# A triangular solution in other temporaries, with the log-decay chain amid its steps, and value, key and gate tiles in another order

## What is computed

```python
proj = h @ w_in
gq, gk, gv, g_low, rw, gate = jnp.split(proj, SPLIT0, axis=-1)
log_decay = jax.nn.log_sigmoid((g_low @ gk_up + gk_bias)) / 16.0
b = jnp.cumsum(g in chunks of 64)                  # GLA decay
q * jnp.exp(b - ref), k * jnp.exp(ref - b)         # ref: middle of the chunk
...
S = S * w_t + sa * b_t + v_t * k_t                 # RWKV-7, token by token
...
o = jnp.concatenate([o_a, o_b]) * jax.nn.silu(gate)
return o @ w_out
```

## Time and profile before

| | us |
|---|---|
| median of three executions | 1244.69 |
| lowest, highest | 1243.75, 1245.27 |
| the profiled execution, its own time | 1252.05 |
| its span, first to last instruction | 1249.8 |
| busy: PE, DVE, ACT, POOL | 1124.4, 662.6, 332.7, 294.0 |
| mean granted TensorE clock | 0.95 of full |

### The profile page before, as it was taken

How to read it: one execution, slowest core, us unless ns; L and a number is a source line. 1 busy time by engine, 2 the same in 40 slices (tenths; PEclk the granted TensorE clock), 3 DMA queues, 4 the chain that set the end, 5 groups by cost and what they waited for, 6 DMA issues and landing times. The chain is left out here.

```text
span 1249.8 us, 20321 instructions
## 1 busy us (share of the span) xinstructions
PE 1124.4 (90%) x8408; PEld 899.1 (72%) x8408; DVE 662.6 (53%) x1031; ACT 332.7 (27%) x749; POOL 294.0 (24%) x190
## 2 busy tenths in 40 slices
PE   3999999999964578898889997999999899998997
PEld 3777777888753468787734446888888788887886
DVE  5288898499995315344434115255510258987233
ACT  6333423101103314233241003011110224554121
POOL 2222322334331011010000004133322534440500
PEclk9999999999987799999989998999999959999999
DMA  5211211632111060200204201111111010131011
GB/s 193 68 51 35 53 49 41 214 101 84 34 51 67 18 186 3 70 3 3 70 1 184 102 34 63 51 42 42 50 50 34 35 51 18 35 133 34 17 51 68
DMA packets 37577, 77.77 MB, mean 62 GB/s; under 512 B 19184, under 2 KB 19712, under 8 KB 37120
## 3 DMA queue, kind: packets, MB, share of 16 engines
q1 hardware_dynamic: 27616, 66.23, 15.9%
q10 hardware_dynamic: 9888, 10.49, 2.6%
HBM read 59.93 MB, written 16.78 MB: 61 GB/s over the span
## 5 line engine op out<-in xcount | busy, mean ns | idle before, releaser
L1383 PE MATMUL ps<-HNH,WH 128*128 128x512 f32 x896 | 356.2, 398 | 51.1 <-ACT GV L508 25.8
L1383 PE MATMUL ps<-HNH,WL 128*128 128x512 f32 x896 | 352.4, 393 | 0.0
L1383 PE MATMUL ps<-HNL,WH 128*128 128x512 f32 x896 | 352.0, 393 | 0.0
L1383 PEld LDWEIGHTS ps<-HNH,WH 128*128 128x128 f32 x896 | 170.4, 190 | 89.9 <-issue 54.4
L1383 PEld LDWEIGHTS ps<-HNH,WL 128*128 128x128 f32 x896 | 170.8, 191 | 36.3 <-issue 1.2
L1383 PEld LDWEIGHTS ps<-HNL,WH 128*128 128x128 f32 x896 | 170.6, 190 | 36.4
L1282 PE MATMUL ps<-BK,SG 128*128 128x512 f32 x256 | 112.8, 601 | 1.4 <-PEq L787 1.4
L1282 PEld LDWEIGHTS ps<-BK,SG 128*128 128x128 f32 x256 | 49.3, 193 | 63.7 <-issue 63.7
L1744 ACT ACTIVATE GV<-GV,nm 128x256 f32<-128x256 f32 x128 | 64.3, 504 | 78.6 <-DVE nm L1765 78.3
L666 DVE TENSOR_TENSOR VQ<-GV 128x62 f32<-128x62 f32 (+30 forms) x62 | 71.4, 1152 | 20.2 <-DMA GV<-bonds_dram 18.1
L1704 PE MATMUL ps<-V,GV 128*128 (+1 forms) x512 | 73.2, 292 | 0.8 <-DVE GV L1778 0.7
(11 more groups left out here) (246 smaller groups left out, 1728.9 us busy)
## 6 DMA issues: line engine op xcount, KB each, us to landing
GV<-in_w1t SPq DMA_DIRECT2D x18, 512.0 KB, 3.6
AR<-in_x SPq DMA_DIRECT2D x16, 512.0 KB, 7.1
WA<-in_w0t SPq DMA_DIRECT2D x16, 512.0 KB, 3.6
RAW<-in_w0t SPq DMA_DIRECT2D x8, 512.0 KB, 3.7
gate_dram<-RAW ACTq DMA_DIRECT2D x8, 512.0 KB, 2.6
SG<-gate_dram SPq DMA_DIRECT2D x1, 4096.0 KB, 15.4
BK<-in_wout SPq DMA_DIRECT2D x4, 1024.0 KB, 6.8
h_dram<-H SPq DMA_DIRECT2D x8, 512.0 KB, 2.6
```

The source lines that it names most:

```text
L1383: last = pe.matmul(out, a, b, start=(k == 0 and i == 0), stop=(k == n - 1 and i == 2))
```

## The change

**Buffers.** `X` moves from `GV` to `XS`, the second half of `VQ`, whose four rows are the temporaries of the pairs (`mixd, kmix, kk, sa`). `TMP` moves to `solve_row`, the first row of `RAW`. Query and key tiles are now kept in `GV`, in the place of the decays they are multiplied with. Value tiles go through `gate_row` to memory (`value_dram`), and are loaded into `VQ` in `chunks0`.

**Order of the tiles.** The low-rank tile is 13, then two gate tiles (14, 15), four value tiles (16 to 19), four query/key tiles (20 to 23), and six gate tiles (24 to 29). All weights from tile 13 on arrive in `WA` alone.

**Engines.** ScalarE keeps the low-rank tile, stores the bonds and loads `X` ahead of the first gate tile. The decay chain's two VectorE parts, `gate_sizes()` and `gate_sums()`, stand within `solve()` before steps 10 and 26. The scan is cut in 16 scans of 64 elements with a mask of one chunk, loaded at the start. GpSimd multiplies each query/key tile with its decay, after the split of the weights two tiles on. SyncE stores the solution instead of ScalarE. In `chunks0` GpSimd clears the states, and TensorE's first transposes no longer wait for `cen`.

```diff
-W0_GATE = 13
-W0_GLOW = 21
-W0_GLA = 22
+W0_GLOW = 13
+W0_VALUE = 16
+W0_QK = 20
+W0_GATES = [14, 15] + list(range(24, 30))
...
-            QK = VQ[:, PAIRS:, :].rearrange("p (a q) t -> p a q t", a=2)
+            XS = VQ[:, PAIRS:, :]
+            QK = GV[:, :, :].rearrange("p (a q) t -> p a q t", a=2)
...
-    X = GV[:, :, :].rearrange("p a t -> p (a t)").rearrange("p (j i) -> p j i", i=C)
-    ST, TMP = kmix, sa
+    X = XS[:, :, :].rearrange("p a t -> p (a t)").rearrange("p (j i) -> p j i", i=C)
+    ST, TMP = kmix, solve_row
+    EARLY, LATE = 10, 26
...
-        return WA[:] if n % 2 == 0 or n == PAIRED else WBK if n < PAIRED else WRAW
+        return WA[:] if n % 2 == 0 or n >= PAIRED else WBK
...
-                sp.wait_ge(parts, 2 * n if n in (PAIRED, PAIRED + 1) else 2 * n - 2)
-                if n == PAIRED + 2:
-                    sp.wait_ge(mixed, PAIRED)
-                if n == PAIRED + 5:
-                    sp.wait_ge(ab_out, 64 * PAIRS)
+                sp.wait_ge(parts, 2 * n if n >= PAIRED else 2 * n - 2)
+                if n == W0_GLOW + 1:
+                    sp.wait_ge(pair_done, PAIRS)
                     sp.dma_start(gk_sb, gkup).then_inc(gk_in, 16)
                 sp.dma_start(arrival(n), w0t[W0_ORDER[n]]).then_inc(w_in[n % 2], 16)
...
+            sp.wait_ge(solved, 2 * (C - 2))
+            sp.dma_start(solved_dram.rearrange("n e p h j i -> (n e p h) j i"), X).then_inc(solved_out, 16)
             sp.wait_ge(solved_out, 16)
-            sp.wait_ge(g_rel, GP)
...
                 split_parts(pool, arrival(n), WH[:, n % 2], WL[:, n % 2], 2 * n, parts)
+                if W0_QK <= n - 2 < W0_QK + 4:
+                    j = n - 2 - W0_QK
+                    pool.wait_ge(tile_kept, n - 1)
+                    pool.wait_ge(g_exp, GP)
+                    pool.tensor_tensor(GV[:, j, :], GV[:, j, :], gate_row, ALU.mult).then_inc(g_scaled, 1)
...
+            def gate_sums():
+                for j in range(GP):
+                    z, l = (nrm, cum)[j], (e2, sw)[j]
+                    dve.wait_ge(gz_step, GP + j + 1)
+                    link(dve.scalar_tensor_tensor(out=z, in0=z, scalar=0.0, in1=l, op0=ALU.min, op1=ALU.subtract))
+                    for c in range(NC):
+                        ins = dve.tensor_tensor_scan(l[:, c * C:(c + 1) * C], chunk_mask[:], z[:, c * C:(c + 1) * C], 0.0,
+                                                     ALU.mult, ALU.add)
+                    link(ins)
+                    relative(l, z, GG[:, j, :])
+                    dve.tensor_copy(mid, mid).then_inc(g_rel, 1)
...
                 for j in range(1, C - 1):
+                    if j == EARLY:
+                        gate_sizes()
+                    if j == LATE:
+                        gate_sums()
...
-            pe.wait_ge(s["consts"], 1)
             turns_av(0)
...
+                if n == 0:
+                    pe.wait_ge(s["consts"], 1)
```

More of the change, by code:

```diff
@@ L485, in _ @@
                     low_rank(p + 1)
-            tile(W0_GATE, W0_GATE % 2)
+            tile(W0_GLOW, W0_GLOW % 2)
             bonds(PAIRS - 1)
-            for n in range(W0_GATE + 1, W0_GLA + 1):
-                tile(n, n % 2)
+            tile(W0_GLOW + 1, (W0_GLOW + 1) % 2)
             pe.wait_ge(glow_kept, 1)
@@ L494, in _ @@
                 for h in range(2):
-                    last = pe.matmul(PS[4 + 2 * j + h][:], gk_sb[:, j * P:(j + 1) * P], mixd[0:16, h * HB:(h + 1) * HB],
+                    last = pe.matmul(PS[4 + 2 * j + h][:], gk_sb[:, j * P:(j + 1) * P], glow[:, h * HB:(h + 1) * HB],
                                      start=True, stop=True)
                 last.then_inc(gz_done, 1)
-            for n in range(W0_GLA + 1, W0_TILES):
+            for n in range(W0_GLOW + 2, W0_TILES):
                 tile(n, n % 2)
@@ L578, in _ @@
             act.activation(small[:, 57:58], small[:, 57:58], ACT.Copy).then_inc(tile_kept, 1)
-            def keep_qk(j):
-                keep(W0_GLA + j, QK[:, j // 2, j % 2, :], ACT.Copy, scale=GLA_SCALE if j < 2 else 1.0)
-            act.wait_ge(gz_done, GP)
[L584 to L590, removed]
+            store_bonds(PAIRS - 1)
+            act.wait_ge(ab_out, 64 * PAIRS)
+            act.wait_ge(mixed, 3 * PAIRS + 1)
+            act.dma_start(X, bonds_dram.rearrange("n e p h j i -> (n e p h) j i")).then_inc(x_in, 16)
+            keep_gate(W0_GLOW + 1)
+            act.wait_ge(gz_done, GP)
             for j in range(GP):
@@ L599, in _ @@
                 act.activation(l, l, ACT.Exp, scale=-1.0).then_inc(gz_step, 1)
-                act.wait_ge(gz_step, 2 * j + 1)
+            for j in range(GP):
+                l = (e2, sw)[j]
+                act.wait_ge(gz_step, GP)
                 act.activation(l, l, ACT.Ln, bias=1.0).then_inc(gz_step, 1)
+            for j in range(4):
+                keep_value(W0_VALUE + j)
             for j in range(GP):
@@ L608, in _ @@
                 act.activation(z, z, ACT.Exp, scale=1.0 / NORMALIZER).then_inc(g_exp, 1)
[L610 removed]
             for j in range(4):
[L612 removed]
+                staged(W0_QK + j)
+                keep(W0_QK + j, gate_row, ACT.Copy, scale=GLA_SCALE if j < 2 else 1.0)
+            for n in W0_GATES[2:]:
+                keep_gate(n)
         @block.vector
@@ L655, in keep_bonds, with gate_sizes @@
                 ins.then_inc(ab_kept, 1)
+            def gate_sizes():
+                for j in range(GP):
+                    z, l = (nrm, cum)[j], (e2, sw)[j]
+                    dve.wait_ge(gz_kept, j + 1)
+                    dve.scalar_tensor_tensor(out=l, in0=z, scalar=-1.0, in1=z, op0=ALU.mult, op1=ALU.max).then_inc(gz_abs, 1)
+            def gate_sums():
+                for j in range(GP):
+                    z, l = (nrm, cum)[j], (e2, sw)[j]
+                    dve.wait_ge(gz_step, GP + j + 1)
[6 more added lines that the diff above has]
+                    dve.tensor_copy(mid, mid).then_inc(g_rel, 1)
             def solve():
@@ L711, in _, with chunks0 @@
             solve()
[L712 to L728, removed]
-def chunks0(nc, sb, sem, ctx, PS, AR, BK, VT, QK, GV, G, GG, small, ident, istack, maska, bdones, TT0, solved_dram,
+def chunks0(nc, sb, sem, ctx, PS, AR, BK, VT, QK, VG, value_dram, value_out, G, GG, small, ident, istack, maska, bdones, TT0, solved_dram,
             solved_out, SG, gla_norm, next_w, w_dram, w_in, gate_dram, gate_out):
@@ L765, in chunks0 @@
     s = {n: sem("c_" + n) for n in names.split()}
-    tt_in = [sem(f"c_tt_in{n}") for n in range(NP)]
+    tt_in = {n: sem(f"c_tt_in{n}") for n in range(2, NP)}
+    vg_in = [sem(f"c_vg_in{h}") for h in range(2)]
     def after(eng, name, n):
@@ L939, in step @@
                 after(pe, "s_kept", 2 * n + e)
+                if n == 0 and e == 0:
+                    pe.wait_ge(s["zeros"], 1)
                 if e == 0:
```

99 lines of the change are left out of this document (60 added, 39 removed).

## The result

The changed kernel takes 1216.1 us (median of four runs, 1212.2 to 1237.1), the kernel before 1244.8 (1243.8 to 1245.3). The ratio is 0.976, 95% interval 0.9733 to 0.9788, some 30 us; it leaves out the run of 1237.1, which had a mean TensorE clock of 0.94 against 0.96 of the others. The forecast was 1219.7, range 1210 to 1228. The profiled execution took 1217.48 us, its span is 1215.7.

The account below looks back on a forecast made before the run. VectorE's solution chain was taken to bound the end of `project0`: 234.6 + 110.8 + 39.3 + 8.3 + 17.2 = 410.2, block 23.4 us earlier. With 1.6 from the loop's start, 1244.7 - 25.0 = 1219.7 us, range 1210 to 1228.

Parts of the forecast that it names:

- What bounds: End of `project0`: TensorE's two stalls, 18.75 us before tile 27 and 25.80 before tile 28, both lead back to VectorE.
- The chain's start: First step of the solution at 234.6 us, with the bond stores ahead of the gate tile.
- The splits: Beside the solution's 62 steps: 14 weight splits by GpSimd, each costing VectorE 2.81 us, 39.3 in all.
- The multiplications: GpSimd's four multiplications inside the solution cost VectorE 2.08 us each, 8.3 us in all.
- The decays: `gate_sizes` and `gate_sums` amid the solution's steps add 17.2 us (13.8 to 20.8), with 4.0 for 16 scans.
- The end: Solution ends at 410.2 us; after store and first chunks' loads the chunk loop's block begins at 422.7, 23.4 us earlier.
- The tile run: TensorE's tiles in `project0` end at 403.5 us, written by 407.2, 15 before the vector chain; tile 14's stall costs nothing.
- The loop: Start of the chunk loop: first products 1.6 us sooner, 0 as lower bound; 3 us allowed for the longer pause.
- The sum: Whole kernel: 23.4 + 1.6 = 25.0 us saved, from 1244.7 to 1219.7 us on the median.
- The clock rival: TensorE stays at 1.2 GHz in the chunk loop after its pause; half the loop gives about 1285 us; 4 in 100.

Follow-up runs that it names:

- The run with 7 splits: Changed kernel with the second part of the decay chain (`gate_sums()`) called after `solve()`; 1278.6 us in one run.
- the run with the small multiplications: Changed kernel with GpSimd's four multiplications acting on 8 of 1024 columns, the rest of the product left out; 1201.0 us in one run.

## Why the prediction was right

The measured time lies inside the range, and the mechanism is the forecast one: the end of VectorE's chain set the block, before and after. That the number came so near is in part luck, as the last two paragraphs here tell.

**What bounds.** Right. One wait for VectorE's chain stood behind both stalls, as the kernel with the first stall taken away shows (47.0 in place of 44.6).

**The chain's start.** 234.6 forecast, 233.8 and 231.4 measured. The steps were right, the load of X varies.

**The splits.** 14 forecast, 14 measured, 2.8 us each. The CAST's share of 0.73 is shown by the run in which ScalarE makes it (some 10.0 us for 14). The run with 7 splits bears out the sum: 132.5 less 2.4 for `gate_sizes` and 7 x 2.81 leaves 110.4 for the steps, where 110.8 was taken.

**The multiplications.** 8.3 us forecast, 6.0 to 6.4 measured: a term mis-sized. 2.08 was the nearest row, but an instruction of 1.17 beside a multiplication took 2.85 and so lost 1.7. The difference is that of the two GpSimd instructions: alone a multiplication takes 2.00 us and a split's subtraction 2.39.

**The decays.** 17.2 us forecast. The sixteen scans took 3.03 us, 0.19 each, where I took 4.0, so the term is 15.2. It lay inside its bounds of 0.14 and 0.36. By the Trainium skill's rule of a fixed part for each instruction (VectorE: DVE Perf Modes, "The TRN2 errata") sixteen scans would take an estimated 4.6, further off; the measurement decides. Each scan by itself lasts 0.26 us in the trace, yet one begins every 0.19: scans that don't wait for each other overlap.

**The end.** The solution was forecast to end at 410.2 and ended at 405.1: 0.8 from the start, 1.9 from the scans, some 2 from the multiplications, 0.2 from `gate_sizes`. The store took 6.9 instead of 6.3, and the block came at 417.7 instead of 422.7: 28.3 us earlier, not 23.4.

**The tile run.** End forecast at 403.5, measured 403.2, with the 5.7 us stall before tile 14. "Costs nothing" was half right: its slack hid it from TensorE's side, but it put one more split beside the solution, 2.6 us in the run without it. The sum counted that split; the argument missed that the stall was its cause. The slack was 10 us and not 15, since the chain ended sooner.

**The loop.** 1.6 us sooner was forecast; at the first transitions it was 0.4 to 1.0, and by the second turn nothing. This step of the prediction failed. The whole loop was as a rule longer than before: from the block to the first output product 185.7 to 189.5 us in the profiles of the changed kernel and its variants, against 185.8 to 186.0 in the three of the kernel before and its variants. The allowance of up to 3 us for it stood in the range and not in the sum. A turn, taken from transitions to transitions, lasts 21.3 us or 22.8 from the second on: the kernel before has two of the longer ones and the changed one two or three; the first turn took 19.7 to 22.2 us in the nine profiles with the new start and 19.5 to 20.0 in the four with the old one. Why is open.

**The sum.** 25.0 us forecast, 28.7 measured on the medians and some 30 by the ratio. Up to the first output product the pair of profiles gives 28.3 - 2.7 = 25.6, and that this is so near 25.0 is luck: 4.9 us too few for the chain and 4.3 too many for the loop cancel. The rest, 3 to 4 us, lies behind the loop, where the change touches nothing. The clock rival did not happen in the loop. A long stretch at 1.2 GHz does occur, but in the attention, before and after the change alike.

## What to carry to other kernels

When one engine's chain sets the end, look for what stretches its instructions from outside: here GpSimd's work was on the path, though GpSimd itself had time, and giving its copies to ScalarE made the solution 10 us shorter and the block 7 us sooner. A small independent chain can be put amid a long dependent one at the price of its instructions, and the place is found from when its result is wanted, with the slack counted at both ends. A store can be split by who needs it first, but follow what waits for the rest of it: issued ahead of the first loads it slowed them, issued behind them it came late for the next stage, and by the loop's end both versions stood alike.

## What the runs showed of the hardware

TensorE's granted clock at the start of layer 1's attention was 0.50 with the engine busy all the time. The stretch differs from execution to execution: the attention took 123.6 us at best, about 125 mostly, 131.5 in four profiles (that of the kernel before among them), and 150.3 in one. Over the runs of the changed kernel the time falls as the mean clock rises, 1238.5 us at 0.940, 1205.5 at 0.970. The clock fell, where it fell, after three short pauses of TensorE at the attention's start. The kernel before, and then the run with the small multiplications (us, PE busy, granted clock, DMA share, GB/s):

```profile
980.00:1000.00 20.00, 16.71 (x90) 0.86 0.16 54
1000.00:1020.00 20.00, 20.00 (x103) 0.50 0.17 53
```

```profile
940.00:960.00 20.00, 16.83 (x86) 1.00 0.12 41
960.00:980.00 20.00, 19.12 (x158) 0.91 0.21 67
980.00:1000.00 20.00, 19.79 (x178) 1.00 0.12 32
```

The pauses add up to much the same in both, 3.3 and 3.2 us in the first windows shown. In the second the clock was at the full level but for a part of one window, in the first it stayed at the lower one with TensorE busy. What decides between the two is open.

Four loads of 128 KB behind a running store of 1.5 MB on the same queue took 9.6 us to the block instead of 5.7. With that store behind them they had landed after 6.3.

A GpSimd CAST of 1024 columns that lasts 1.04 us alone cost VectorE's chain 0.7 us, a subtraction of 2.39 us cost it 2.1, and a multiplication of 2.00 us cost it 1.5 to 1.7. The same CAST on ScalarE cost it nothing that the timeline shows.
